# A mixture-of-experts stage in float32: shift by columns, four units of weights in idle buffers, two experts written out

## The reference

```python
def expert_choice_ffn(h, w_router, w1, w3, w2):
    n, d = h.shape[1], h.shape[2]
    cap = CAPACITY_FACTOR * n // N_EXPERTS          # 2 * 256 // 16 = 32
    aff = jax.nn.softmax((h @ w_router).astype(jnp.float32), axis=-1)
    gate, idx = lax.top_k(jnp.swapaxes(aff, 1, 2), cap)
    xe = jax.vmap(lambda hb, ib: hb[ib])(h, idx)
    hid = jax.nn.silu(jnp.einsum('becd,edf->becf', xe, w1)) * jnp.einsum('becd,edf->becf', xe, w3)
    ye = jnp.einsum('becf,efd->becd', hid, w2) * gate[..., None].astype(h.dtype)
    def scatter(yb, ib):
        return jnp.zeros((n, d), h.dtype).at[ib.reshape(-1)].add(yb.reshape(-1, d))
    return jax.vmap(scatter)(ye, idx)

# h is modulate(x, g_ffn, shift, scale) = rmsnorm(x, g_ffn) * (1 + scale) + shift
```

## Time and profile before

| | |
|---|---|
| median of 3 runs | 2968.07 us (2967.51 to 2973.12) |
| profiled execution | 2980.04 us |
| its span, first to last instruction | 2978.3 us |
| TensorE busy | 2795.8 us (94%) |
| weight loads of TensorE | 2179.7 us (73%) |
| VectorE, ScalarE, GpSimd busy | 523.7, 358.7, 71.0 us |
| read from HBM | 691.85 MB |
| mean granted TensorE clock | 0.904 of full |

### The profile page before, as it was taken

One profiled execution on the slowest core, in us unless ns is written; L12 is line 12 of the kernel. 1 busy time (PEld: TensorE's weight loads), 2 busy tenths in 40 slices (PEclk: granted clock), 3 DMA queues, 4 the chain that ended last, 5 costly groups with the idle time before them and its releaser, 6 DMA issues. The chain is left out here.

```text
span 2978.3 us, 34705 instructions
## 1 busy us (share of the span) xinstructions
PE 2795.8 (94%) x15057; PEld 2179.7 (73%) x15057; DVE 523.7 (18%) x1134; ACT 358.7 (12%) x796; POOL 71.0 (2%) x87
## 2 busy tenths in 40 slices
PE   7999889989988998999998899999999998899999
PEld 5675455545544555888886788888888886788888
DVE  1421000010010001111223411111111224411111
ACT  2320010110011001000112301000000112301000
POOL 0000000000000000000200000000000200000000
PEclk9987777777787678999998999999999998999999
DMA  9547999999999999345552144445345552144340
GB/s 361 195 170 320 426 428 429 430 428 428 428 428 428 415 429 391 113 142 163 162 165 92 57 142 160 138 155 166 131 148 163 158 178 77 58 168 142 128 155 29
DMA packets 250666, 694.23 MB, mean 233 GB/s; under 512 B 12897, under 2 KB 194513, under 8 KB 225873
## 3 DMA queue, kind: packets, MB, share of 16 engines
q1 hardware_dynamic: 248112, 688.54, 61.1%
q10 hardware_dynamic: 2464, 4.39, 0.4%
HBM read 691.85 MB, written 1.05 MB: 233 GB/s over the span
## 5 line engine op out<-in xcount | busy, mean ns | idle before, releaser
L1068 PE MATMUL banks<-ZT,ring 128*128 128x256 f32 x2816 | 625.2, 380 | 1.3 <-ACT ZT L1524 1.3
L1068 PEld LDWEIGHTS banks<-ZT,ring 128*128 128x128 f32 x2816 | 535.7, 191 | 75.7 <-issue 1.8
L1084 PE MATMUL banks<-ZP,ring 128*128 128x256 f32 x1408 | 316.9, 379 | 0.0
L979 PE MATMUL banks<-ring,BK 128*32 128x512 f32 x2048 | 239.3, 613 | 61.4 <-DMA ring<-in_w 37.1
L1084 PEld LDWEIGHTS banks<-ZP,ring 128*128 128x128 f32 x1408 | 267.5, 190 | 36.4
L1281 PE MATMUL banks<-ZT,ring 128*128 128x256 f32 x1024 | 238.3, 387 | 0.0
L979 PEld LDWEIGHTS banks<-ring,BK 128*32 128x32 f32 x2048 | 66.4, 111 | 221.5 <-issue 126.3
L1281 PEld LDWEIGHTS banks<-ZT,ring 128*128 128x128 f32 x1024 | 197.3, 195 | 27.9 <-issue 0.4
L2012 DVE TENSOR_TENSOR ZP<-banks,RB 128x512 f32<-128x512 f32 x88 | 60.9, 692 | 686.7 <-PE banks L1068 686.5
L1004 PE MATMUL banks<-ring,GB 128*32 128x512 f32 x1024 | 179.9, 852 | 0.0
L1567 ACT ACTIVATE ZP<-ZP 128x256 f32<-128x256 f32 x88 | 36.6, 416 | 839.2 <-DVE ZP L2012 839.2
(11 more groups left out here) (339 smaller groups left out, 2214.2 us busy)
## 6 DMA issues: line engine op xcount, KB each, us to landing
ring<-in_w SPq DMA_DIRECT2D x192, 2048.0 KB, 18.0
ring<-in_w_in SPq DMA_DIRECT2D x79, 1024.0 KB, 5.0
ring<-in_ffn_w_gate SPq DMA_DIRECT2D x44, 1024.0 KB, 5.2
ring<-in_ffn_w_up SPq DMA_DIRECT2D x44, 1024.0 KB, 7.6
ring<-in_ffn_w_down SPq DMA_DIRECT2D x44, 1024.0 KB, 4.8
ring<-in_w_mod SPq DMA_DIRECT2D x24, 1024.0 KB, 11.6
ring<-in_w_branch SPq DMA_DIRECT2D x16, 1024.0 KB, 6.2
ring<-in_w_out SPq DMA_DIRECT2D x12, 1024.0 KB, 5.0
```

The lines of the kernel that those rows point to most:

```text
L979: last = mm(ps[32 * j:32 * j + 32, 4 + b, :], XE[:, k, :], slot(n)[:, 512 * b:512 * b + 512], start=(k < 4), stop=(k >= 4))
L1068: last = mm(ps[:, 4 + q % 4, 256 * w:256 * w + 256], slot(n + w)[:, 256 * k + P * (q % 2):256 * k + P * (q % 2) + P], ZT[:, k, :], start=( ...
L1084: last = mm(ps[:, c // 2, 256 * (c % 2):256 * (c % 2) + 256], slot(n + 2)[:, D * (q % 2) + P * c:D * (q % 2) + P * c + P], FH[:, q % 4, :] ...
```

## The change

- **Shift by columns.** The shift is turned once into a column tile `BP` (128 x 8, in `small`) by four narrow products, and added by DVE as it copies the gathered rows to `XE` (`tensor_tensor` in place of a copy). `BROW`, its eight transposes and the eight products for each gather go. DVE waits for `bias_out` once.
- **Four units aside.** Units 20 to 23 of the first expert (half of `w2`) are loaded to four buffers that are idle by then: `YF`, the upper half of `QT`, `ZT`, and the upper half of `ZP`. Each load stands in SyncE's queue behind a wait for the last reader of its buffer. Ring places 8 to 11 are passed over in the first expert's second half, and the counts that are waited for at places 8 and 10 are 16 lower from then on. `SQ` of the first norm moves to `SQ0` in `PB`, since `YF` is taken.
- **First and last expert written out.** The loop runs over 14 experts. The first scatter starts the accumulation itself (`start=` for every second chunk), the zero tile, its memset and its products go. The last expert gathers nothing and its scatter ends the accumulation; `moe_full` is released bank by bank, and DVE updates chunks 0 and 1 after the first.

The diff, cut to its core:

```diff
+ASIDE = 20
+ASIDE_PLACES = (8, 10)
...
-        def wait_unit(eng, n, turns=0):
+        def wait_unit(eng, n, turns=0, past=False):
             paired = 16 * 2 * NE if n >= U_LAYER and n % 2 else 0
-            eng.wait_ge(landed[n % RING], turns * 16 + 16 * (n // RING + 1) - paired)
+            aside = 16 if (past or n >= U_LAYER) and n % RING in ASIDE_PLACES else 0
+            eng.wait_ge(landed[n % RING], turns * 16 + 16 * (n // RING + 1) - paired - aside)
...
+        BP = small[:, 440:448]
+        SQ0 = PBf[:, 0:2048].rearrange("p (c t) -> p c t", c=KC)
+        aside = [YF[:, 0:UNIT], QT[:, UNIT:2 * UNIT], ZTf, ZP[:, UNIT:2 * UNIT]]
...
+            def load_aside(i):
+                r0 = 1024 + 512 * (i // 2)
+                sp.dma_start(aside[i].rearrange("p (j n) -> p j n", j=2),
+                             w2[r0:r0 + 512, :].rearrange("(p i j) n -> p i j n", i=2, j=2)[:, i % 2]).then_inc(aside_in, 16)
+            for u in range(0, 6, 2):
+                load_in(u, 0)
+            sp.wait_ge(unit_done, U_WIN + 4)
+            load_aside(0)
+            sp.wait_ge(gm_full, 2)
+            load_aside(1)
+            for u in range(6, 10, 2):
+                load_in(u, 0)
+            sp.wait_ge(unit_done, U_ROUTER)
+            load_aside(2)
+            load_in(10, 0)
+            sp.wait_ge(unit_done, U_ROUTER + 1)
+            load_aside(3)
+            for u in range(12, 16, 2):
+                load_in(u, 0)
+            for u in range(0, ASIDE - 16, 2):
+                load_down(u, 0)
+            with sp.Fori(1, NE) as e:
...
-            for k in range(KC):
-                last = mm(ps[0:1, 4 + k // 4, P * (k % 4):P * (k % 4) + P], scaleB[:, 2, k:k + 1], ident, start=True, stop=True)
+            for i in range(2):
+                for h in range(2):
+                    last = mm(ps[64 * h:64 * h + 64, 7, 32:40].rearrange("p (j i) -> p i j", i=2)[:, i, :],
+                              ident.rearrange("p (q i) -> p i q", i=2)[:, i, :],
+                              scaleB[:, 2, :].rearrange("p (j h) -> p h j", h=2)[:, h, :], start=True, stop=True)
...
-            pe.wait_ge(zeros_set, 1)
...
-            for b in range(4):
-                mm(ps[:, b, :], ident, zeros, start=True, stop=False, skip_group_check=True)
...
-                        mm(ps[:, 5, 32 * k:32 * k + 32], Z[:, t, P * k:P * k + P], OH[:, t, :], start=(t == 0), stop=False)
-                    last = mm(ps[:, 5, 32 * k:32 * k + 32], BROW[:, P * k:P * k + P], ones[0:1, 0:CAP], start=False, stop=True)
+                        last = mm(ps[:, 5, 32 * k:32 * k + 32], Z[:, t, P * k:P * k + P], OH[:, t, :],
+                                  start=(t == 0), stop=(t == TT - 1))
...
+                    of_aside = first and 16 + u >= ASIDE
+                    if of_aside:
+                        pe.wait_ge(aside_in, 16 * 4)
...
-                gather_turn(e + 2)
+                if not last_one:
+                    gather_turn(e + 2)
...
-                gather(e + 2)
+                if not last_one:
+                    gather(e + 2)
...
-                              start=False, stop=False, skip_group_check=True)
-                last.then_inc(scattered, 1)
-            for b in range(4):
-                last = mm(ps[:, b, 0:1], ident, zeros[:, 0:1], start=False, stop=True, skip_group_check=True)
-            last.then_inc(moe_full, 1)
+                              start=(first and c % 2 == 0), stop=last_one, skip_group_check=True)
+                    if last_one and c % 2:
+                        last.then_inc(moe_full, 1)
...
+            expert(0, first=True)
+            with pe.Fori(1, NE - 1) as e:
+                expert(e)
+            expert(NE - 1, last_one=True)
...
-                copy(XE, ps[:, 5, 0:256].rearrange("p (k s) -> p k s", k=KC)).then_inc(xe_ready, 1)
+                tt(XE, ps[:, 5, 0:256].rearrange("p (k s) -> p k s", k=KC), over(BP, CAP), ALU.add).then_inc(xe_ready, 1)
...
-                    dve.wait_ge(moe_full, 1)
                     dve.wait_ge(fin_cols, 1)
                     for c in range(KC):
+                        dve.wait_ge(moe_full, c // 2 + 1)
```

More of the change, by code:

```diff
@@ L235, in build @@
         landed = [sem(f"unit_landed{i}") for i in range(RING)]
+        aside_in = sem("aside_in")
         unit_done = sem("unit_done")
@@ L741, in square_sums @@
                 for t in range(TT):
-                    last = mm(ps[:, 6, t:t + 1], SQ[:, 0, P * t:P * t + P], ones[:, 0:1], start=True, stop=True)
+                    last = mm(ps[:, 6, t:t + 1], (SQ if v else SQ0)[:, 0, P * t:P * t + P], ones[:, 0:1], start=True, stop=True)
                 last.then_inc(sums_out, 1)
@@ L968, in _, with expert @@
             gather(1)
-            with pe.Fori(0, NE) as e:
+            def expert(e, first=False, last_one=False):
                 def parts(w):
@@ L975, in parts @@
                         if n % 2 == 0:
-                            wait_unit(pe, U_EXPERT + n, e * 2)
+                            wait_unit(pe, U_EXPERT + n, e * 2, not first)
                         for b in range(4):
@@ L998, in down @@
                         pe.wait_ge(ht_ready, e * 2 + (u // 4 + 1))
-                    if u % 2 == 0:
-                        wait_unit(pe, U_EXPERT + 16 + u, e * 2)
+                    of_aside = first and 16 + u >= ASIDE
+                    if of_aside:
+                        pe.wait_ge(aside_in, 16 * 4)
+                    elif u % 2 == 0:
+                        wait_unit(pe, U_EXPERT + 16 + u, e * 2, not first)
+                    w = aside[16 + u - ASIDE] if of_aside else slot(16 + u)
                     for i in range(2):
@@ L1889, in _ @@
             own(copy(BR, ps[:, 7, 16:16 + NE]))
[L1890 to L1891 removed]
+            copy(BP, ps[:, 7, 32:40]).then_inc(bias_out, 1)
             def gained(v, c, dst, gain):
@@ L1949, in gathered, with expert @@
                 dve.wait_ge(xe_full, done)
-                copy(XE, ps[:, 5, 0:256].rearrange("p (k s) -> p k s", k=KC)).then_inc(xe_ready, 1)
+                tt(XE, ps[:, 5, 0:256].rearrange("p (k s) -> p k s", k=KC), over(BP, CAP), ALU.add).then_inc(xe_ready, 1)
+            dve.wait_ge(bias_out, 1)
             select(idxcol[:, 0:1], 0)
             gathered(1)
-            with dve.Fori(0, NE) as e:
-                select(nextcol[:, bass.ds(e, 1)], e + 1)
+            def expert(e, last_one=False):
+                if not last_one:
+                    select(nextcol[:, bass.ds(e, 1)], e + 1)
                 dve.wait_ge(scattered, e)
@@ L1966, in _ @@
                        ALU.mult).then_inc(ht_ready, 1)
-                gathered(e + 2)
+                if not last_one:
+                    gathered(e + 2)
                 wait_done(dve, U_EXPERT + 23, e * 2)
                 copy(YE[:, 512:1024], ps[:, 7, :]).then_inc(ye_v, 1)
+            with dve.Fori(0, NE - 1) as e:
+                expert(e)
+            expert(NE - 1, last_one=True)
             for l in range(NL):
@@ L2356, in rstd_of @@
             def rstd_of(v):
+                sq = SQ if v else SQ0
                 for c in range(1, KC):
                     pool.wait_ge(squares_out, v * KC + c + 1)
-                    last = nc.gpsimd.tensor_tensor(SQ[:, 0, :], SQ[:, 0, :], SQ[:, c, :], ALU.add)
+                    last = nc.gpsimd.tensor_tensor(sq[:, 0, :], sq[:, 0, :], sq[:, c, :], ALU.add)
                     if c < KC - 1:
```

28 lines of the change are left out of this document (14 added, 14 removed).

## The result

| | before | after |
|---|---|---|
| median, same chip, 4 runs each | 2970.6 us (2967.5 to 2983.7) | 2947.0 us (2939.6 to 2949.6) |
| profiled execution, and its span | 2980.0, 2978.3 us | 2949.6, 2947.8 us |
| TensorE busy, its weight loads | 2795.8, 2179.7 us | 2695.5, 2081.8 us |
| mean granted TensorE clock | 0.904 | 0.915 |

What follows compares the result with a forecast made beforehand. The prediction held that the stream of weight transfers bounds the expert stage, at 428 GB/s. Its terms, 2.5 + 1.8 + 6.6 + 2.7 + 15.9 = 29.5 us, cut the median of 2968.07 to 2938.6 us, range 2926 to 2951.

Steps and rivals of the forecast that it cites:

- Part 1, turning the shift: At the router's bias: eight narrower instructions replace 16 that take 3.57 us; 2.5 us gained, 0.8 to 3.5.
- the 2 us named as the sign: At the turning of the shift: the new instructions should take under 2 us if the forecast is right.
- Part 2, zero products and first gather: Ahead of the experts: first gather at the low clock but without row products, 8.1 us for 10.2; 1.8 us gained.
- Part 3, four units aside: First two experts: four units fewer to stream, 9.8 us, less holes in the traffic; 6.6 us gained.
- The hole of 3 us: First expert: the weight stream stops for 2.9 us because the next pair must wait for its slots.
- Part 4, gathers in the loop: Loop: each gather loses 4.5 us of row products, which pays only where the queue ran dry; 2.7 us, 0 to 4.
- Part 5, the end: Last expert to first dense product: no gather, faster down units and scatter, earlier residual update; 15.9 us gained, or 13.
- No hole and a fast gather: Rival, first gather and expert stage: the clock's phase is kind, 37.8 us gained, 2930 us; 13%.
- The low clock takes part of it back: Rival: projection's start, first down product and last scatter run slow; 20.3 us gained, 2948 us; 16%.
- the second hole: Second expert: the stream runs dry for 0.4 us before pair 12 can be issued.
- Units aside for nothing: Rival, expert stage: later pairs wait as long as they ran ahead; 20.2 us left, 2948 us; 4%.
- TensorE as the loop's bound: Rival, loop: slower products make each of 14 turns last 64.2 us instead of 58.8; 3014 us; 3%.

Runs made afterwards that it cites:

- e2: The changed kernel with the shift as a row again: eight transposes, and eight more products in each gather; 0.9965 of the kernel before.
- e5: The kernel before with the shift added by columns and nothing else changed; 0.9923 of the kernel before.
- e8: The changed kernel with four 512-column products of constants while VectorE searches, where the zero products stood; 0.987 of the kernel before.
- e12: The same kernel as e8, run a second time; 0.9879 of the kernel before.
- e6: The changed kernel with eight idle narrow products in each gather of the loop, not in the first gather; 0.9924 of the kernel before.
- e10: The changed kernel with idle narrow products in the loop's gathers and no units aside, all in the ring; 0.9948 of the kernel before.
- e1: The changed kernel run again without any edit; 2941.8 us over 6 runs, 0.9887 of the kernel before.
- e3: The changed kernel with all 24 units of the first expert in the ring, none aside; 0.9906 of the kernel before.
- e4: The changed kernel, but the last expert gathers again as before; 0.9903 of the kernel before.
- e7: The changed kernel with the ring run on without a gap past the units aside; 0.9883 of the kernel before.
- e9: The changed kernel with both the ring run on without a gap and 512-column products during the search; 0.9881 of the kernel before.
- e11: The changed kernel, but the residual update waits for the whole last scatter; one run, 2954.2 us.

## Why the prediction was right, point by point

- **What bounds the kernel.** Right. TensorE lost 72 us of work in the expert stage and the stage 5.5.
- **Part 1, turning the shift.** 2.5 forecast, 2.1 measured (9.7 to 7.6); L945 takes 0.60 us, under the 2 us named as the sign. Not forecast were 1.2 us more up to the end of the search: the router's products run 3.7 us there, 5.1 before. Every kernel with columns has 43.0 to 43.8 us in this stretch, before and e2 have 44.5 each, so it comes with the columns; by what way was not tested.
- **Part 2, zero products and first gather.** 1.8 forecast, 2.9 measured. Mechanism right: low clock throughout, and the zero products had paid for the high one (e5, e8, e12). The block came out at 7.1/8 = 0.88 us, where I took 0.99 from a row that had the row products between its blocks.
- **Part 3, four units aside.** 6.6 forecast, 5.6 timed with overlapping intervals, 4.3 and 5.5 by the traces. The hole of 3 us is in its place. The second hole was 0.9 for 0.4.
- **Part 4, gathers in the loop.** The step that failed in size: "2.7 us with a small one near 360; 0 to 4". It counted the holes of one trace, and it took the gather to be 4.5 us longer by its row products, where e2's turn beside after's shows 6.9 us in the gather and 3.9 more in the down units and the scatter behind it, which then run at the low level. The idle products of e6 put the price of the longer gather at 11 us and those of e10 at 12.5, each known to some 8 us, with 12.5 and 10.4 in the traces' expert stages. The mechanism, a queue run dry behind a gather at the low clock, was right; how much it costs in other executions of the kernel before was not traced, and no run shows that trace to be the usual one. Against that one trace the part is worth no more than its 2.8 us of closed holes, and e5's stage is indeed 2.7 us shorter. That the forecast held with this term is in part luck.
- **Part 5, the end.** 15.9 forecast, 13.3 and 15.9 in the two traces. Scatter 3.69 us for 3.7, dense product 3.5 us behind it for 3.7. What after has less than e1 lies ahead of the steps I summed: its last up products and its sums all run at the low level, of which before, like e1, had a part at the high one (1.92 and 1.94 us for the first runs of each). The 9.6 for the gather were booked on writing the last expert out; 5.8 of them belong to the columns.
- **The sum.** By edit, the columns were 2.5 + 4.6 + 2.7 + 5.8 = 15.6 us in my terms and are 23 timed; the units aside 6.6, and 5.6; writing out the rest, 29.5 - 15.6 - 6.6 = 7.3, and is 33 - 23 - 5.6 = about 4, with 33 as the mean of 31.5 and 34. The errors, +7, -1 and -3, partly cancelled: the total was nearer than its parts. With some 8 us of uncertainty on each they could also be smaller.
- **The rivals.** No hole and a fast gather: falls, the hole is there and the gather slow. The low clock takes part of it back: only in the first gather, which the forecast had counted, and at the last expert in one of the two traces, by 2.6 us; in the first turn (granted clock 0.70 from 267 to 284 us) what shows of it is the second hole, 0.9 for 0.4. Units aside for nothing: falls by e3. TensorE as the loop's bound: falls for the changed kernel (plateau of 428), but e2, e6 and e10 show how near it lay, with single turns of 64 to 66 us.

## What to carry to other kernels

Where a stream of weights sets the pace, the work of an engine is hidden only as long as it frees buffers in time in its unluckiest turn; look for the places where the traffic falls, and do not price a stall from one execution: here the price read from one trace was 3 us, and idle work of the same length cost about 11. A head start for the stream can be given back in the consumer's first turns, so look at what those turns take, at which level of the clock they run and where buffers stay empty, before it is lengthened. Work that lengthens a narrow chain can cost more than its own time, when what stands behind it then runs at the low level. Before dead products are removed ahead of a short chain of narrow ones, see whether the clock behind them was theirs.

## What the runs showed of the hardware that was not expected

Code that no experiment touches takes different times from execution to execution. The dense layers behind the experts take 1793.8 to 1796.5 us in nine traces (before, after, e1, e4, e7, e8, e9, e11, e12) and 1782.1 to 1784.8 in five (e2, e3, e5, e6, e10), and no trace lies between. The same stretch in after and in e3 (windows, columns as above):

```profile
2434.00:2504.00 70.00, 57.55 (x339) 47.92 (x336) 32.73 (x82) 18.61 (x69) 0.73 (x2) 0.83 0.19 60
```

```profile
2440.00:2510.00 70.00, 56.96 (x360) 47.37 (x361) 34.55 (x82) 22.35 (x82) 0.00 (x0) 0.93 0.19 60
```

TensorE and VectorE do nearly the same work in both, at granted clocks of 0.83 and 0.93. No kernel was traced in both groups, so that this goes with the execution and not with the kernel is argued and not shown. What speaks for it: the profiled executions of the five were the lowest or second lowest of their kernel's 6 to 12 runs (e2: 2955.4 at a median of 2967.7), those of e1, e4, e7, e8, e9 and e12 the highest or second highest. So where in the dense layers the granted clock is low goes with 10 to 12 us of this kernel, as much as e6's idle products cost in the loop, and profiled executions can only be compared stretch by stretch. The one of before lay in the long group, which would account for the 12 us by which it stood above the first median. The start of the kernel up to the router's bias differs too, with no edit in it: 166.4 to 167.8 us in eight traces and 169.9 to 172.0 in six; after and e1 lie in the first group and e8, e11 and e12, with the same code up to there, in the second, so here it is spread.
